# A Trainium2 kernel of two transformer blocks: stage inputs, squares and memory parts placed 64 bytes further in SBUF

## The chip, the cores and the metric

One core of one Trainium2 chip runs the whole program in one launch. The metric is the device time of that core in microseconds (us); lower is better. Before the change it is 3032.66 us, the median of 3 runs (3022.43 to 3038.39).

## The reference, cut to what matters

Everything is float32. The input is x with 256 tokens of 1024 features. A first block runs two layers of (FFN, mixer of four branches, FFN). A second block runs four layers of (mixer, cross-attention over 256 memory tokens, FFN); its mixers are differential attention, HGRN2, a chunked gating unit, and differential attention again. The cost is in products of activations (256 tokens) with weights. The FFN, of which there are eight in all, shows the pattern:

```python
def swiglu(h, w_gu, w_down):
    gate, up = jnp.split(h @ w_gu, 2, axis=-1)
    return (jax.nn.silu(gate) * up) @ w_down
...
        x = x + mem_cross_attention(rmsnorm(x, norm_cross[i]), mem_n, ca_w_q[i], ca_w_kv[i], ca_w_o[i])
        x = x + swiglu(rmsnorm(x, norm_ffn[i]), ffn_w_gu[i], ffn_w_down[i])
```

In each FFN the hidden width is 2816, so the first product has 2 x 2816 output features and the second 2816 input features.

## The kernel before, in words

**Three products for one.** Each float32 operand is cut into a high part, rounded to the type fp32r, and a low part, the rounded remainder. One product of a 128x128 block becomes three matmuls into the same PSUM accumulator, issued by `product` (L432 to L438): low weight or activation part times high (L435), high times low (L436), high times high (L437). Each is one load of a stationary operand (128x128, shown as engine PEld) and one matmul that streams a moving operand of 256 columns (PE). In the profile's names the moving operand stands first and the stationary second: `G<-ah,wl` streams `ah` against loaded `wl`. Projections by `features` (L440) and the FFN's `down` (L569) stream activations against loaded weights; projections by `tokens` (L473) and `tokens_by_input` (L461) stream weights against loaded activations.

**The weights' ring.** The weights come in 460 units of 128x2048 float32 (1 MB) through a ring of five slots. For each unit the SP queue waits until PE has finished the unit five places earlier (`unit_done`, L371) and starts the DMA into `raw` (L372); ACT makes the high part `wh` (L1053) four units ahead of PE; POOL (GpSimd) makes the low part `wl` in place over `raw` (L387); PE waits on `low_ready` and does 48 matmuls for the unit.

**The stages.** Eight FFN stages (`ffn`, L530) have 22 units in the first product, whose moving operands are the stage input parts `ah` and `al`, and 11 units in the second (`down`, L569), whose moving operands are the gated product's parts `gh` and `gl`. Two `mix1` stages, the four mixers and the four cross-attentions use `ah`/`al` for the stage input, `mh`/`ml` for branch outputs or the memory's parts, and `oh`/`ol`, `hoh`/`hol`, `soh`/`sol` for the input of an output projection. At the start of a stage ACT cuts x to `ah` (L1092) and DVE makes `al` (L1688), in four pairs, and PE takes up each pair as it is ready (`features_by_input`, L449). ACT squares x into `full` (L1104) and PE sums those (L514, L517) for the norm, after the second unit of the stage. Evacuations of the first product run on DVE (L1819, L1821, L1824, L1827, L1829) and ACT (L1204).

**Where things lie.** `sb` (L134) hands out byte offsets within each of the 128 partitions, one tensor after the other. All pieces that a matmul or load takes begin at multiples of 512 bytes from the start of their tensor, so that the remainder of a tensor's offset holds for every piece. The program's first free byte is 16481; L141 rounds it up to 16512, which is 129 x 128. With the widths in `sb`'s calls, the offsets of the tensors that matter are:

| tensors | offset before | remainder by 128 | by 256 | offset after | remainder by 128 | by 256 |
|---|---|---|---|---|---|---|
| raw and wl | 16512 | 0 | 128 | 16512 | 0 | 128 |
| wh | 57472 | 0 | 128 | 57472 | 0 | 128 |
| x | 98432 | 0 | 128 | 98432 | 0 | 128 |
| ah | 106624 | 0 | 128 | 106688 | 64 | 192 |
| al | 114816 | 0 | 128 | 114880 | 64 | 192 |
| full | 123008 | 0 | 128 | 123072 | 64 | 192 |
| mh | 131200 | 0 | 128 | 131264 | 64 | 192 |
| ml | 139392 | 0 | 128 | 139456 | 64 | 192 |
| decays (a part of con) | 150912 | 0 | 128 | 150976 | 64 | 192 |
| work: gh, gl, oh, ol and the like | 163648 | 64 | 64 | 163776 | 64 | 192 |
| lh, ll (in work, 32768 further) | 196416 | 64 | 64 | 196544 | 64 | 192 |

The other tensors of `work` (`prob1`, `z`, `cum`, all with remainder 96 by 128) keep their remainder by 128; `ones`, `ident` and the masks go from 0 to 64 with `full`. The last tensor ends at 229312 bytes after the change, under the limit of 229368.

Of the kernel before, what the change touches and what calls it, by code (L numbers as in the profile page):

```python
# [128 lines left out]
def build(nc, w_units, params_d, consts_d, hot_d, rel_d, x_d, mem_d, ws_d, bs_d, out_d,  # L129
          table_d, units=UNITS, stop_after=None):  # L130

    at = [nc.sbuf_base]

    def sb(name, width, dt=F32, offset=None):  # L134

        if offset is None:
            offset = at[0]
            at[0] += (4 * width + 31) // 32 * 32
        return nc.alloc_sbuf_tensor_at(name, [P, width], dt, offset=offset)
# [3 lines left out]
    wl = sb("wl", RING * UW, F32R, offset=at[0] - 4 * RING * UW)  # L143
    wh = sb("wh", RING * UW, F32R)
    x = sb("x", KD * T)
    acts_at = at[0]
    ah = sb("ah", KD * T, F32R)
    al = sb("al", KD * T, F32R)
# [8 lines left out]
    root = sb("root", 4 * T + 8)  # L157
    rr = root[:, 3 * T:4 * T + 2]
    small = sb("small", 136)
    work_at = at[0]  # L160
    WORK = 12288
    work = sb("work", WORK)
# [2603 lines left out]
def program(nc, arrays, **kw):  # L2766
    args = [nc.dram_tensor(k, list(a.shape), F32, kind="ExternalInput").ap() for k, a in arrays.items()]
    args.append(nc.dram_tensor("out", [P, KD * T], F32, kind="ExternalOutput").ap())
    args.append(nc.dram_tensor("tables", [12, P, PERIOD], F32, kind="Internal").ap())
    build(nc, *args, **kw)  # L2770
# [12 lines left out]
```

How the kernel before makes its waits and increments, by code:

```python
        @block.sync  # L356
        def _(sp):
            sp.dma_start(par[:, :], params_d).then_inc(par_in, 16)
            for k in range(KD // 2):
                sp.dma_start(x[:, k * 512:(k + 1) * 512], x_d[:, k * 512:(k + 1) * 512]).then_inc(x_in[k], 16)
            sp.dma_start(raw[:, 0:UW], w_units[0, :, :]).then_inc(raw_landed[0], 16)
            sp.dma_start(onehot[0:NB + 1, :], hot_d).then_inc(tables_in, 16)
            sp.dma_start(rel[0:NB + 1, 0:12], rel_d).then_inc(tables_in, 16)
            for n in range(1, RING):
                sp.dma_start(raw[:, n * UW:(n + 1) * UW], w_units[n, :, :]).then_inc(raw_landed[n], 16)
            sp.dma_start(con[:, :], consts_d).then_inc(consts_in, 16)
            with sp.Fori(1, units // RING) as i:
                for j in range(RING):
                    sp.wait_ge(unit_done, RING * i + (j + 1 - RING))
                    sp.dma_start(raw[:, j * UW:(j + 1) * UW], w_units[i * RING + j, :, :])\
                        .then_inc(raw_landed[j], 16)
            for c2 in range(KD // 2):
                sp.wait_ge(result, c2 + 1)
                sp.dma_start(out_d[:, 512 * c2:512 * (c2 + 1)], full[:, 512 * c2:512 * (c2 + 1)])\
                    .then_inc(stored, 16)
            sp.wait_ge(stored, 16 * (KD // 2))
# [4 lines left out]
            def low(n, j):  # L384
                pool.wait_ge(high_ready, n + 1)
                pool.tensor_tensor(wl[:, j * UW:(j + 1) * UW], raw[:, j * UW:(j + 1) * UW],
```

## Time and profile before

| | us |
|---|---|
| median of 3 runs | 3032.66 |
| lowest and highest run | 3022.43, 3038.39 |
| the profiled execution's own time | 3031.32 |
| its span in the trace | 3029.5 |
| PE busy in it | 2922.5 |
| POOL busy | 2123.0 |
| ACT busy | 1328.3 |
| DVE busy | 1131.8 |

The span is the trace's first to last instruction; 1.8 us of the execution's own time lie outside it. Matmuls overlap their neighbours in the trace: each is shown as lasting some 280 ns while the next begins 110 to 120 ns later, so the pace of PE is read from the starts, not from the durations. The clock column of a window (PEclk) is the share of full TensorE speed that the chip granted, 1.00 for 2.4 GHz and 0.50 for 1.2 GHz.

### The profile page before, as it was taken

What the parts mean: (1) busy time and instruction counts of PE and PEld (TensorE: products, weight loads), DVE (VectorE), ACT (ScalarE), POOL (GpSimd) and SP (SyncE); (2) the same over time, 40 slices, a digit from 0 to 9 for tenths busy, and PEclk for the clock granted to TensorE, in tenths of its full rate; (3) what the DMA queues carried; (4) which work ended last, traced back from release to release, by engine and by line L of the source; (5) the groups of instructions that cost most, each with busy time, mean ns of one, the idle gap of its engine ahead of it and who ended that gap; (6) DMA issues with size and microseconds to landing.
All of it is one profiled execution on the core that took longest, in us unless ns stands there. A gap on an engine that the chain in (4) does not pass through costs nothing.

```text
span 3029.5 us, 56111 instructions
## 1 busy us (share of the span) xinstructions
PE 2922.5 (96%) x24276; PEld 2866.2 (95%) x24276; DVE 1131.8 (37%) x1810; ACT 1328.3 (44%) x1473; POOL 2123.0 (70%) x464
## 2 busy tenths in 40 slices
PE   7999999999999999999999999999998999999998
PEld 7999889999998899999999998999998999999998
DVE  2326544223165343245242226343134431353421
ACT  4344534343345344355443475443354433454432
POOL 5887558778866477866678682668876488756685
PEclk9999989999999899999999999999999999999999
DMA  6554335555544254544345541445553355434453
GB/s 224 190 194 160 140 125 177 185 181 181 192 163 147 105 194 169 195 167 154 140 167 182 181 169 66 144 153 181 181 195 140 126 184 192 170 143 147 158 186 116
DMA packets 73441, 496.89 MB, mean 164 GB/s; under 512 B 8027, under 2 KB 12763, under 8 KB 14084
## 3 DMA queue, kind: packets, MB, share of 16 engines
q1 hardware_dynamic: 67768, 485.88, 45.0%
q10 hardware_dynamic: 5452, 7.62, 1.0%
q8 instruction: 192, 3.15, 0.4%
q14 instruction: 29, 0.24, 0.0%
HBM read 490.05 MB, written 3.41 MB: 163 GB/s over the span
## 4 chain that ended last, share of the span: by engine, by line
PE 85%; DVE 6%; DMA 3%; issue 3%; ACT 2%; POOL 2%; SPq 0%; DVEq 0%; POOLq 0%; ACTq 0%
PE G L435 21%; PE G L436 21%; PE G L437 21%; PE S L437 5%; PE S L435 5%; PE S L436 5%; DMA raw<-w_units 3%; DVE al L1688 3%; POOL wl L387 2%; PE G L634 1%; PE S L983 1%; ACT wh L1053 1%; PE S L514 1%; PE S L517 0%; PE S L782 0%
## 5 line engine op out<-in xcount | busy, mean ns | idle before, releaser
L387 POOL TENSOR_TENSOR wl<-raw,wh 128x2048 fp32r<-128x2048 f32 x460 | 2122.8, 4624 | 877.2 <-ACT wh L1053 862.3
L1053 ACT ACTIVATE wh<-raw 128x2048 fp32r<-128x2048 f32 x456 | 871.6, 1913 | 1096.8 <-DMA raw<-w_units 1096.5
L435 PE MATMUL G<-ah,wl 128*128 128x256 f32 x4304 | 1235.7, 287 | 44.2 <-DVE al L1688 36.0
L436 PE MATMUL G<-al,wh 128*128 128x256 f32 x4304 | 1228.0, 285 | 0.0
L437 PE MATMUL G<-ah,wh 128*128 128x256 f32 x4304 | 1227.4, 285 | 0.0
L435 PEld LDWEIGHTS G<-ah,wl 128*128 128x128 f32 x4304 | 836.0, 194 | 57.2 <-DVE al L1688 28.7
L436 PEld LDWEIGHTS G<-al,wh 128*128 128x128 f32 x4304 | 836.3, 194 | 0.1
L437 PEld LDWEIGHTS G<-ah,wh 128*128 128x128 f32 x4304 | 836.0, 194 | 0.0
L435 PE MATMUL S<-gh,wl 128*128 128x256 f32 x1408 | 388.9, 276 | 0.0
L436 PE MATMUL S<-gl,wh 128*128 128x256 f32 x1408 | 388.9, 276 | 0.0
L437 PE MATMUL S<-gh,wh 128*128 128x256 f32 x1408 | 388.8, 276 | 0.0
L435 PEld LDWEIGHTS S<-gh,wl 128*128 128x128 f32 x1408 | 264.4, 188 | 0.0
L436 PEld LDWEIGHTS S<-gl,wh 128*128 128x128 f32 x1408 | 264.4, 188 | 0.0
L437 PEld LDWEIGHTS S<-gh,wh 128*128 128x128 f32 x1408 | 264.3, 188 | 0.0
L1821 DVE TENSOR_TENSOR G<-G,root 128x512 f32<-128x512 f32 x88 | 61.4, 698 | 369.8 <-PE G L437 369.8
L1850 DVE SCALAR_TENSOR_TENSOR x<-S,x 128x512 f32<-128x512 f32 x32 | 21.9, 685 | 408.8 <-PE S L437 408.8
L1688 DVE SCALAR_TENSOR_TENSOR al<-x,par,ah 128x256 fp32r<-128x256 f32 x144 | 168.3, 1213 | 15.5 <-ACT ah L1092 15.4
L1092 ACT ACTIVATE ah<-x,par 128x256 fp32r<-128x256 f32 x144 | 64.5, 500 | 175.9 <-DVE x L1768 140.9
L1819 DVE TENSOR_TENSOR G<-G,root 128x512 f32<-128x512 f32 x88 | 61.4, 698 | 190.4 <-PE G L437 190.1
L435 PE MATMUL G<-mh,wl 128*128 128x256 f32 x384 | 110.0, 286 | 3.2 <-ACT kc L1171 1.7
L435 PE MATMUL G<-wh,al 128*128 128x256 f32 x384 | 109.2, 284 | 4.0 <-DVE ll L2453 2.2
L436 PE MATMUL G<-wl,ah 128*128 128x256 f32 x384 | 108.7, 283 | 0.0
(357 smaller groups left out, 3873.1 us busy)
## 6 DMA issues: line engine op xcount, KB each, us to landing
raw<-w_units SPq DMA_DIRECT2D x460, 1024.0 KB, 4.8
bias<-tables ACTq DMA_DIRECT2D x24, 128.0 KB, 4.4
tables<-trow ACTq DMA_DIRECT2D x1, 1536.0 KB
con<-consts SPq DMA_DIRECT2D x1, 1056.0 KB, 18.2
x<-x_in SPq DMA_DIRECT2D x4, 256.0 KB, 5.2
memx<-mem_in ACTq DMA_DIRECT2D x1, 1024.0 KB, 4.8
out<-full SPq DMA_DIRECT2D x4, 256.0 KB, 2.5
tables<-trow ACTq DMA_DIRECT2D x1, 768.0 KB
```

The source lines that it names most:

```text
L387: pool.tensor_tensor(wl[:, j * UW:(j + 1) * UW], raw[:, j * UW:(j + 1) * UW], wh[:, j * UW:(j + 1) * UW].bitcast(F32), ALU.subtract)\
L435: pe.matmul(out, sl, vh, start=start and k == 0, stop=False, **kw)
L436: pe.matmul(out, sh, vl, start=False, stop=False, **kw)
L437: ins = pe.matmul(out, sh, vh, start=False, stop=stop and k == len(parts) - 1, **kw)
L514: pe.matmul(out[:, 0:T], ones[:, 0:P], full[:, k * T:(k + 1) * T], start=k == 0, stop=k == 1)
L634: ins = pe.matmul(out, v_of(kc), pt[:, kc * 512 + n * P:kc * 512 + (n + 1) * P], start=kc == 0, stop=kc == nk // P - 1)
L983: ins = pe.matmul(out[:, h * T:(h + 1) * T], qf[:, f * T + g * P:f * T + (g + 1) * P], kc[:, f * T:(f + 1) * T], start=dc == 0, stop=dc == 1)
L1053: act.activation(wh[:, j * UW:(j + 1) * UW], raw[:, j * UW:(j + 1) * UW], ACT.Copy)\
L1092: ins = act.activation(ah[:, q * T:(q + 1) * T], x[:, q * T:(q + 1) * T], ACT.Copy, scale=pcol(gain, q))
L1688: ins = dve.scalar_tensor_tensor(al[:, q * T:(q + 1) * T], x[:, q * T:(q + 1) * T], pcol(gain, q), ah[:, q * T:(q + 1) * T].bitcast(F32), ...
L1819: dve.tensor_tensor(pairs(gate), pairs(gate), along, ALU.mult).then_inc(scaled, 1)
L1821: dve.tensor_tensor(pairs(value), pairs(value), along, ALU.mult).then_inc(up_scaled, 1)
```

## The change

Two lines are added to the layout. The first moves everything from `ah` on by 64 bytes; the second sets the start of `work` to the next offset that leaves 64 by 128, which was its remainder already. No instruction, wait, transfer or size is different; only the addresses are.

```diff
     wl = sb("wl", RING * UW, F32R, offset=at[0] - 4 * RING * UW)
     wh = sb("wh", RING * UW, F32R)
     x = sb("x", KD * T)
+    at[0] += 64
     acts_at = at[0]
     ah = sb("ah", KD * T, F32R)
     al = sb("al", KD * T, F32R)
...
     small = sb("small", 136)
+    at[0] = (at[0] + 63) // 128 * 128 + 64
     work_at = at[0]
```

## Rows read from the trace of the kernel before

**Rows 1.** The page: busy us, share of the span and instructions by engine.
```profile
PE 2922.5 (96%) x24276; PEld 2866.2 (95%) x24276; DVE 1131.8 (37%) x1810; ACT 1328.3 (44%) x1473; POOL 2123.0 (70%) x464
```

**Rows 2.** What PE waited for, over the whole span; us, times, longest.
```profile
PE G L435 <- DVE al L1688: 37.8, 23, 3.4
...
PE G L634 <- DVE pt L1917: 8.7, 4, 3.6
...
PE G L435 <- POOL wl L387: 3.5, 4, 2.0
```

**Rows 3.** PE's instruction groups, shapes apart: busy us, mean ns, idle before.
```profile
L437 PE MATMUL G<-ah,wh 128*128 128x256 f32 x4304 | 1227.4, 285 | 0.0
...
L437 PE MATMUL S<-gh,wh 128*128 128x256 f32 x1408 | 388.8, 276 | 0.0
...
L437 PE MATMUL G<-wh,ah 128*128 128x256 f32 x384 | 108.7, 283 | 0.0
...
L437 PE MATMUL G<-mh,wh 128*128 128x256 f32 x384 | 108.6, 283 | 0.0
...
L437 PE MATMUL G<-oh,wh 128*128 128x256 f32 x384 | 106.7, 278 | 0.0
...
L437 PE MATMUL G<-wh,mh 128*128 128x256 f32 x256 | 72.5, 283 | 0.0
...
L437 PE MATMUL S<-mh,wh 128*128 128x256 f32 x128 | 36.2, 283 | 0.0
```

**Rows 4.** Tile view of ah, gh and oh, one stretch each: count, first and last start.
```profile
L435 PE MATMUL G<-ah,wl x279: 283/283/284, 679.7 to 779.8; 128*128 128x256 f32 x140
...
L435 PE MATMUL S<-gh,wl x119: 275/276/277, 159.8 to 199.9; 128*128 128x256 f32 x119
...
L435 PE MATMUL G<-oh,wl x54: 276/276/277, 1499.8 to 1517.8; 128*128 128x256 f32 x54
```

**Rows 5.** Windows of these stretches: PE busy, then PEclk, DMA share, GB/s.
```profile
680.00:780.00 100.00, 100.00 (x836) 100.00 (x835) 30.59 (x44) 37.30 (x27) 85.33 (x19) 1.00 0.51 182
160.00:200.00 40.00, 40.00 (x356) 40.00 (x355) 0.00 (x0) 15.23 (x8) 33.24 (x8) 1.00 0.53 186
...
1412.00:1432.00 20.00, 20.00 (x172) 20.00 (x172) 7.45 (x8) 8.15 (x9) 11.51 (x4) 1.00 0.56 206
```

**Rows 6.** The tile view of ah where weights stream (1796 to 1812 us).
```profile
L436 PE MATMUL G<-wl,ah x45: 283/283/284, 1795.9 to 1811.7; 128*128 128x256 f32 x45
```

**Rows 7.** Timeline of PE, the first matmuls with decays: start us, us.
```profile
1816.27 0.28 PE L875 MATMUL S<-decays,lh 128*128 128x256 f32 x1
...
1817.97 0.28 PE L876 MATMUL S<-decays,ll 128*128 128x256 f32 x1
```

**Rows 8.** The tile view of oh in the first differential attention (1412 to 1432 us).
```profile
L435 PE MATMUL G<-oh,wl x57: 280/281/282, 1412.1 to 1431.8; 128*128 128x256 f32 x57
```

**Rows 9.** Timeline of PE at an FFN's start at the lower clock: start us, us.
```profile
1718.10 0.41 PE L436 MATMUL G<-al,wh 128*128 128x256 f32 x1
...
1720.66 0.41 PE L436 MATMUL G<-al,wh 128*128 128x256 f32 x1
```

**Rows 10.** The cores view: span in us and mean granted clock.
```profile
core 0: 3029.5 us, clock 0.985
```

**Rows 11.** Windows of the first FFN and the third.
```profile
40.00:110.00 70.00, 66.25 (x544) 65.30 (x544) 20.41 (x31) 23.88 (x18) 46.50 (x11) 1.00 0.68 199
640.00:835.00 195.00, 193.44 (x1641) 193.16 (x1640) 53.10 (x75) 78.94 (x62) 156.37 (x34) 1.00 0.52 184
```

**Rows 12.** The tile view of raw, 700 to 780 us: the supply of weights.
```profile
L387 POOL TENSOR_TENSOR wl<-raw,wh x15: 4614/4621/4634, 696.2 to 775.5; 128x2048 fp32r<-128x2048 f32 x15
...
DMA to landing us min/median/max: 4.7/4.8/7.0
```

**Rows 13.** The tile views of soh and mh: ns min/median/max of their making.
```profile
L1642 DVE TENSOR_TENSOR sol<-full,soh x4: 678/678/4512, 2275.4 to 2281.1; 128x512 fp32r<-128x512 f32 x4
...
L2011 DVE TENSOR_TENSOR ml<-full,mh x4: 691/693/1099, 370.2 to 1056.0; 128x512 fp32r<-128x512 f32 x4
```

## The prediction

> **What bounds the kernel now.** I read the page's busy times first: PE is busy for 2922.5 of 3029.5 us, POOL for 2123.0, ACT and DVE for less than half [rows 1]. The view of waits says how little PE stands still: its largest item is 37.8 us in 23 waits for DVE's `al` at the starts of stages, the others are a few us each [rows 2]. So PE is the bound nearly everywhere, and the question is at what pace it works while it never waits. The durations of the groups hint at an answer: matmuls that stream `ah` or `mh` against weights last 283 to 285 ns, those that stream `gh` 276, those that stream `oh` 278 [rows 3]. As durations overlap, I take the pace from first and last starts. From 679.7 to 779.8 us there are 279 matmuls of L435 on `ah`, each followed by two more of its product: 100.1 us / 278 / 3 = 120.0 ns per matmul. For `gh` it is 40.1 / 118 / 3 = 113.3 ns, for `oh` after 1500 us 18.0 / 53 / 3 = 113.2 ns [rows 4]. PE is busy without a break in the stretches of `ah` and `gh` and the granted clock is 1.00 in both (2.4 GHz), so neither a wait nor the clock makes the difference [rows 5].
>
> What differs is the remainder of the two SBUF operands by 128 bytes. `ah` and the weights both leave 0, `gh` and `oh` leave 64 against the weights' 0. Two more pairs help to tell whether the moving operand alone decides. Where weights stream against a loaded `ah`, again 0 with 0, the pace is 15.8 / 44 / 3 = 119.7 ns [rows 6]. Where `decays` (0) streams against a loaded `lh` or `ll` (64), 16 matmuls start within 1.70 us, 1.70 / 15 = 113.3 ns [rows 7]. It is the pair that counts: equal remainders cost 6.7 ns a matmul, different ones do not, whichever side has the 64. One stretch does not fit: the output projection of the first differential attention also streams `oh`, and runs at 19.7 / 56 / 3 = 117.3 ns [rows 8] at a granted clock of 1.00 [rows 5].
>
> **The change, part by part.** It removes no instruction and adds none. The first line gives `ah`, `al`, `full`, `mh`, `ml` the remainder 64; the second keeps `gh`, `oh` and the rest of the working area at 64. So the pairs of 0 with 0 become 64 with 0.
>
> Their number: per form (4304 + 384 + 384 + 256 + 128) products with `ah` or `mh` on either side = 5456, times three matmuls = 16368 [rows 3]. Not all run at 120 ns. After the wait at a stage's start the clock falls to its lower level, and the matmuls then start 2.56 / 12 = 213 ns apart [rows 9]. The mean clock of 0.985 [rows 10] leaves 0.015 x 2 x 3029.5 = 91 us at the lower level; if all of that were such matmuls it would be some 430. I leave 400 out, as part of it is other work. The gross gain is 15970 x (120.0 - 113.3) = 107 us. In an FFN that is 22 x 48 x 6.7 ns = 7.1 us of some 190 [rows 11].
>
> What of it is lost:
> - *Starts of stages.* There PE takes the pairs of `ah`/`al` as DVE gives them, 23 waits [rows 2]. What PE saves in the first unit, 48 x 6.7 = 0.32 us, partly becomes waiting. Between 0 and 23 x 0.32 = 7.4 us; I take 4, since the first wait is often the long one and the rest of the unit runs free.
> - *Cover inside the mixers.* Units of weights cover the work of DVE and ACT on attention and decays, and PE already waits at the end of some, 4 times for `pt` [rows 2]. With the smaller items of that view I count some 30 such waits. Each loses at most one unit's 0.32 us, 0 to 9.6 in all; I take 3, because most waits last well under 1 us and several follow fp32 matmuls that keep their pace.
> - *The first FFN.* There weights arrive late: PE is busy for 66.25 us of 70 [rows 11]. Units that PE leaves earlier ask for weights earlier, so something between nothing and the whole 7.1 us is lost; I take 3.
> - *Supply elsewhere.* A unit now takes 48 x 120 = 5.76 us of PE and would take 5.44. POOL needs 4.62 per unit and a transfer lands after 4.8 [rows 12]; `down` works at 5.44 per unit already, at 186 GB/s and without a wait [rows 5]. I take 0; if the cover failed, PE would wait for `wl` as in the first FFN (3.5 us in 4 waits [rows 2]).
> - *Pairs that become equal.* `decays` goes to 64 and meets `lh` and `ll` at 64: 128 matmuls x 6.7 = 0.9 us, a loss. `ones` and `full` move together and stay equal; the transposes stream or load fp32, where I see no such pace in the trace and take 0.
> - *DVE and ACT on the moved tiles.* The subtraction that makes `sol` from tiles of different remainder takes 678 ns, that of `ml` from equal ones 693 [rows 13]. So both signs are possible, 15 ns an instruction. Only the first two `al` of a stage lie on the path: under 1 us in all, taken as 0.
>
> The sum: 107 - 4 - 3 - 3 - 1 = 96 us. The profiled execution took 3031.3 us, which gives 2935; its time is 1.4 us under the median shown, so I say **2936**.
>
> A rule speaks against all this. The Trainium skill, in SBUF — State Buffer, section "SBUF: two separate sides", says that TensorE, ScalarE and VectorE's own port pair never wait on anyone, and it names no effect of addresses on the two reads of TensorE. By that rule the change gives 0 and the time stays 3033; the two paces in this trace do not agree with it. A second page, TensorE: Matmul & The Clock Gate, section "Back-to-back issue gap", gives 262 cycles at full clock for 256 columns, an estimate of 109.2 ns; by that the gross gain could be 172 us, but no long stretch here goes under 113.
>
> **The rivals.**
> *Part of PE's time falls into the pace of 117.3 ns* that `oh` shows although its remainders differ [rows 8]. Against it: the eight `down` phases and the other output projections hold 113. If all the moved pairs ran so, the gain would be 15970 x 2.7 = 43 us less 8 of losses, 2998; if half did, 2967.
> *No change.* The pace may hang on something else that separates the tiles, such as how far apart or how high they lie. Then the time stays at 3033. For it: `gh`, `oh`, `lh` all lie in the upper working area. Against it: `decays`, 0 by 128, lies just above `ml` and is fast only because its partner is elsewhere; the rule of the skill would end here too.
> *Slower: the remainder that counts is that by 256.* The weights leave 128, `gh` leaves 64 now and 192 after. If the fast pairs are those where the streamed operand is 64 below the weights, and 64 above is as slow as equal, then `ah` gains nothing and the products with `gh` and the `oh` family fall back: (1408 + 384 + 64 + 64) x 3 = 5760 matmuls x 6.7 = 39 us, a time of 3071. It decides if a streamed operand 64 above its partner is slow. `decays` is 64 above `lh` by 256 and ran at 113.3 [rows 7], but those are only 16 matmuls.
>
> **How the numbers follow.** The main case, the pace of 113 nearly everywhere, gets 0.82; the pace of 117 for much of the work 0.10; no change 0.05; slower 0.03. About 0.5% (15 us) is what a measurement of this kernel can tell from no change. The first two cases are faster by more than that: 0.92. The range: without any loss the profiled 3031.3 - 107 = 2924, and runs of one kernel lie up to 10 us under their median, so 2915; upward the upper bounds of the losses (7.4 + 9.6 + 7.1 + 1 = 25) give 2950, and the case of half the work at 117 gives 2967, so I close at 2976. Left out are full 117, no change and slower, about 0.15.
>
> **What would show it.** In the profile after, the tile view of `ah` in a window of an FFN should give 113.3 ns per matmul and durations of 276; tokens' matmuls the same; `gh` and `oh` as before, `decays` with `lh` 120. An FFN should last 7 us less, PE's busy time fall to about 2820, its waits grow by 5 to 20 us, and POOL's busy time stay at 2123. `ah` at 120 would refute the reading of remainders, `gh` at 120 would show the rule by 256, and a large wait for POOL or DMA would show supply as the next bound.

## The result: 1.6% faster, half of what was forecast

The changed kernel takes 2982.36 us (median of 4 runs, 2981.16 to 2983.62) against 3031.06 us for the kernel before: the ratio is 0.9837, with a 95% interval of 0.9818 to 0.9856. The forecast was 2936 us with a range of 2915 to 2976, so the direction was right and the size, 49 us instead of 95, was not.

The page of the changed kernel (line numbers are two higher than before) shows busy times and the largest groups of PE, then DVE's group for `al`:

```profile
PE 2895.0 (97%) x24276; PEld 2840.8 (95%) x24276; DVE 1105.2 (37%) x1810; ACT 1328.5 (45%) x1473; POOL 2125.6 (71%) x464
...
L439 PE MATMUL G<-ah,wh 128*128 128x256 f32 x4304 | 1207.1, 280 | 0.0
...
L439 PE MATMUL S<-gh,wh 128*128 128x256 f32 x1408 | 393.0, 279 | 0.0
...
L1690 DVE SCALAR_TENSOR_TENSOR al<-x,par,ah 128x256 fp32r<-128x256 f32 x144 | 139.3, 1012 | 12.9 <-ACT ah L1094 12.7
```

Against [rows 1] PE is busy for 27.5 us less, while the matmuls of the group that streams `ah` last 280 ns instead of the 285 of [rows 3], and those of `gh` 279 instead of 276. The paces stand in the tile views, here of `ah` from 700 to 780 us and from 219 to 228 us, of `ah` where weights stream (from 1752 us), and of `gh` from 160 to 200 us:

```profile
L437 PE MATMUL G<-ah,wl x228: 280/280/280, 699.7 to 779.9; 128*128 128x256 f32 x114
...
L437 PE MATMUL G<-ah,wl x28: 276/276/276, 218.7 to 227.9; 128*128 128x256 f32 x28
...
L438 PE MATMUL G<-wl,ah x54: 276/276/276, 1751.8 to 1769.9; 128*128 128x256 f32 x54
...
L437 PE MATMUL S<-gh,wl x114: 279/279/279, 159.8 to 199.7; 128*128 128x256 f32 x114
```

In the long stretches the matmuls on `ah` now start every 80.2 / 227 / 3 = 117.8 ns. Some short stretches, the second row shows one, go at 9.2 / 27 / 3 = 113.6 ns; they hold 850 of the 12912 matmuls that stream `ah`. Streamed weights against a loaded `ah` go at 18.1 / 53 / 3 = 113.8 ns here; and `gh`, which was at 113.3 ns [rows 4], goes at 39.9 / 113 / 3 = 117.7 ns. The granted clock is full in both long stretches, as the windows show:

```profile
700.00:780.00 80.00, 80.00 (x682) 80.00 (x681) 24.90 (x36) 31.13 (x22) 67.10 (x15) 1.00 0.51 185
160.00:200.00 40.00, 40.00 (x342) 40.00 (x341) 0.00 (x0) 13.98 (x8) 32.86 (x8) 1.00 0.52 184
```

The third difference stands in PE's waits. Where 37.8 us in 23 waits went to `al` before [rows 2], the changed kernel has:

```profile
PE G L437 <- DVE al L1690: 12.5, 17, 1.3
...
PE G L636 <- DVE pt L1919: 8.9, 4, 3.8
...
PE G L437 <- POOL wl L389: 6.2, 5, 2.7
```

**The ledger.** I took the distance between the starts of every pair of consecutive matmuls in the two traces. Of the 16368 matmuls on moved tiles some 16000 run without a wait and at full clock; their mean fell from 119.93 to 117.20 ns, a gain of 16000 x 2.73 = 44 us. The 5720 others of the `gh` and `oh` family rose from 113.7 to 117.8 ns, a loss of 23 us. The waits for `al` fell by 25 us. The distances on moved tiles that show the lower clock in whole or in part (131 to 230 ns) fell from 311 to 238; at some 95 ns more than a matmul at full clock that is 7 us. Together 53 us, and the spans differ by 49.7: the waits for POOL grew by 2.7 us [rows 2], and the rest is spread over small items. So only 44 - 23 = 21 us of the gain come from the pace of the matmuls, which is what the change aimed at; 32 us come from the starts of stages.

### The profile page after: what moved, and what is told of

Same layout as the page of the kernel before. It is cut to its first block, busy times and chain, and to the rows that moved or that the text cites. A ratio compares the mean times of both kernels' runs of the same rounds, so it can differ in the third digit from the quotient of the medians.

```text
span 2979.8 us, 56111 instructions
## 1 busy us (share of the span) xinstructions
PE 2895.0 (97%) x24276; PEld 2840.8 (95%) x24276; DVE 1105.2 (37%) x1810; ACT 1328.5 (45%) x1473; POOL 2125.6 (71%) x464
## 4 chain that ended last, share of the span: by engine, by line
PE 85%; DVE 5%; issue 3%; DMA 3%; ACT 2%; POOL 2%; SPq 0%; POOLq 0%; DVEq 0%; ACTq 0%
PE G L437 21%; PE G L439 21%; PE G L438 21%; PE S L437 5%; PE S L439 5%; PE S L438 5%; DMA raw<-w_units 3%; DVE al L1690 2%; POOL wl L389 2%; PE G L636 1%; PE S L985 1%; ACT wh L1055 1%; PE S L516 1%; PE S L519 0%; PE S L784 0%
## 5 line engine op out<-in xcount | busy, mean ns | idle before, releaser
L437 PE MATMUL G<-ah,wl 128*128 128x256 f32 x4304 | 1217.8, 283 | 22.4 <-DVE al L1690 11.3
L438 PE MATMUL G<-al,wh 128*128 128x256 f32 x4304 | 1207.7, 281 | 0.0
L439 PE MATMUL G<-ah,wh 128*128 128x256 f32 x4304 | 1207.1, 280 | 0.0
L437 PEld LDWEIGHTS G<-ah,wl 128*128 128x128 f32 x4304 | 815.8, 190 | 34.5 <-issue 24.4
L439 PEld LDWEIGHTS G<-ah,wh 128*128 128x128 f32 x4304 | 816.1, 190 | 0.0
L438 PEld LDWEIGHTS G<-al,wh 128*128 128x128 f32 x4304 | 813.9, 189 | 0.1
L1690 DVE SCALAR_TENSOR_TENSOR al<-x,par,ah 128x256 fp32r<-128x256 f32 x144 | 139.3, 1012 | 12.9 <-ACT ah L1094 12.7
L437 PE MATMUL G<-oh,wl 128*128 128x256 f32 x384 | 107.8, 281 | 0.0
```

The source lines that it names most:

```text
L437: pe.matmul(out, sl, vh, start=start and k == 0, stop=False, **kw)
L438: pe.matmul(out, sh, vl, start=False, stop=False, **kw)
L439: ins = pe.matmul(out, sh, vh, start=False, stop=stop and k == len(parts) - 1, **kw)
L1690: ins = dve.scalar_tensor_tensor(al[:, q * T:(q + 1) * T], x[:, q * T:(q + 1) * T], pcol(gain, q), ah[:, q * T:(q + 1) * T].bitcast(F32), ...
```

## The experiments

Addresses or small matters of order differ in these kernels, and one (g_entry_mm) has a few matmuls more. The time of each is given with its ratio to the kernel before, run beside it. The expectations name their theories by letters and say what each holds. Distances of tiles are given here by 256 bytes, from the weights, which are never moved: "64 above" for 64 more than the weights, "64 below" for 64 less. In the kernel before `ah` is level with the weights and `gh` 64 below; in the changed kernel both are 64 above. The second line of the change, which keeps 64 by 128, moved `gh` by 128 bytes to the other side.

### The working area alone

```diff
     small = sb("small", 136)
+    at[0] += 128
     work_at = at[0]
```

> Only the working area moves, by 128 bytes: ah leaves 128 by 256 like the weights, gh and oh leave 192. Theory A (side): ah at 120, gh and oh at 117.8, 26 us more than the kernel before, about 3057. Theory B (entry): gh enters from the pace of 120 as before and takes 113.3, about 3031.

Measured: 3023.12 us, ratio 0.9958 (0.9934 to 0.9982), beside 3035.64 for the kernel before. The tile view of `gh` from 160 to 200 us and PE's wait for `al`:

```profile
L436 PE MATMUL S<-gh,wl x114: 280/280/280, 159.8 to 199.7; 128*128 128x256 f32 x114
```

```profile
PE G L436 <- DVE al L1689: 12.9, 17, 1.5
```

As theory A says, `gh` is at 39.9 / 113 / 3 = 117.7 ns, in all eight FFNs, although it is entered from the pace of 120 as before. `ah` stays at 120. So the side on which `gh` lies decides its pace, and the remainder by 128 can't be the whole rule. The time was missed by both theories: matmuls that are 24 us slower in sum gave a kernel 12.5 us faster than before. What paid for it is the wait for `al`, 12.9 us where it was 37.8, without a change to `ah`, `al` or x, and fewer matmuls at the lower clock behind these waits.

**Why slower matmuls shorten that wait** can be followed at the stage that starts near 1520 us. First DVE and POOL in the kernel before, as timelines (start us, us); the second row is the last of the four `al` of the first:

```profile
1520.63 7.88 DVE L1688 SCALAR_TENSOR_TENSOR al<-x,par,ah 128x256 fp32r<-128x256 f32 x4
...
1523.74 4.77 DVE L1688 SCALAR_TENSOR_TENSOR al<-x,par,ah 128x256 fp32r<-128x256 f32 x1
```

```profile
1518.11 4.63 POOL L387 TENSOR_TENSOR wl<-raw,wh 128x2048 fp32r<-128x2048 f32 x1 [0.84 <-ACT wh L1053]
1523.54 9.41 POOL L387 TENSOR_TENSOR wl<-raw,wh 128x2048 fp32r<-128x2048 f32 x2 [0.79 <-ACT wh L1053]
```

then the same place with the working area moved:

```profile
1537.29 3.36 DVE L1689 SCALAR_TENSOR_TENSOR al<-x,par,ah 128x256 fp32r<-128x256 f32 x4
...
1540.16 0.48 DVE L1689 SCALAR_TENSOR_TENSOR al<-x,par,ah 128x256 fp32r<-128x256 f32 x1
```

```profile
1534.55 4.62 POOL L388 TENSOR_TENSOR wl<-raw,wh 128x2048 fp32r<-128x2048 f32 x1 [1.02 <-ACT wh L1054]
1540.20 4.95 POOL L388 TENSOR_TENSOR wl<-raw,wh 128x2048 fp32r<-128x2048 f32 x1 [1.02 <-ACT wh L1054]
```

The four `al` of the last two pairs take 7.88 us in the one and 3.36 in the other. In both, the third pair can't go on before POOL's subtraction ends (1522.74 and 1539.17). In the kernel before POOL starts its next one at 1523.54, 0.20 us ahead of the last `al`, which stands still until it ends. With the other pace the output projection's units are 5.65 us apart instead of 5.44, POOL starts at 1540.20, 0.04 us behind the last `al`, and nothing stands still. PE then also doesn't fall to the lower clock there. The Trainium skill (SBUF — State Buffer, "SBUF: two separate sides") describes this lock: a DVE instruction with two SBUF inputs and a GpSimd instruction that reads SBUF exclude each other for their whole length. The trace agrees: an `al` of 0.47 us lasts 4.77 when POOL is first. The kernel before loses this race at six stage starts, each time by 0.18 to 0.20 us; the changed kernel loses it at none, but wins it at ten of them by only 0.02 us, which is luck and no design.

### The race by itself

In the kernel before, with its own addresses, ACT makes the last owed high part behind the squares, so that POOL is released later (cut to its core):

```diff
-                    if owed[0] and owed[0] >= KD // 2 - k:
+                    if owed[0] and owed[0] >= KD // 2 - k and k < KD // 2 - 1:
                         owed[0] -= 1
                         step()
...
+                if owed[0]:
+                    owed[0] -= 1
+                    step()
                 if unit[0] + LEAD < units:
```

> The kernel before with its own addresses; in cut_input ACT makes the weights' high part that is owed behind the last pair only after the squares, some 2.2 us later, so that POOL's subtraction starts behind DVE's last al. Theory D (a race at the start of six stages: POOL starts 0.2 us before DVE's last pair and holds it up for 3.7 us, and PE then does some 17 matmuls at the lower clock): the waits for al fall from 38 us in 23 to about 13 us, each of the six starts gains 3.7 + 1.6 = 5.3 us, 32 us in all, about 3001. Rival E (the changed addresses themselves made DVE or POOL faster there): nothing changes, about 3033.

Measured: 2996.64 us, ratio 0.9887 (0.9861 to 0.9912), 36.7 us less than the kernel before.

```profile
PE G L435 <- DVE al L1691: 17.3, 17, 2.2
```

The paces are those of the kernel before (`ah` 120.0, `gh` 113.4 in every FFN), and the wait is 17.3 us. So the race alone was worth 37 us of the kernel before. That the changed kernel got most of that by being slower elsewhere is what the ledger's 32 us and the experiment before this one say together; no run takes the race out of the changed kernel itself.

### Both sides for both tiles

`root`, `small` and `pick2` are moved ahead of `ah`; their 4800 bytes bring `ah` 64 below the weights without padding, and `gh` stays 64 below.

```diff
     x = sb("x", KD * T)
+    root = sb("root", 4 * T + 8)
+    rr = root[:, 3 * T:4 * T + 2]
+    small = sb("small", 136)
+    pick2 = sb("pick2", 28)
     acts_at = at[0]
```

> root, small and pick2 are moved ahead of ah; no byte is added. ah, mh and full then leave 64 by 256 (they left 128 before, 192 after the change), the weights 128, the working area with gh and oh 64 as before the change. Theory A, the side counts: a streamed operand 64 below its loaded partner by 256 goes at 113.3 ns, one 64 above at 117.8. Then ah, mh, gh and oh run at 113.3, the products that stream weights at 117.8, and the time is about 2905 to 2930 us, the upper end if the long waits for al of the kernel before return. Theory B, only entry counts: with remainders 64 apart on either side both paces hold once taken, most restarts take 117.8, and gh takes over what ah has. Then ah and gh stand mostly at 117.8 and the time is about 2982. Theory C, the forecast's, equal or not by 128: nothing differs from the changed kernel, 2982.

Measured: 3001.0 us, ratio 0.9901 (0.9869 to 0.9933). None of the three theories holds as it stood. `gh` runs at 40.1 / 118 / 3 = 113.3 ns in four FFNs and at 50.2 / 142 / 3 = 117.8 ns in the other four, and always at the pace that `ah` had just before it. Two of its down phases, the first and the second:

```profile
L435 PE MATMUL S<-gh,wl x119: 276/276/276, 169.8 to 209.9; 128*128 128x256 f32 x119
...
L437 PE MATMUL S<-gh,wh x143: 281/281/281, 599.7 to 649.9; 128*128 128x256 f32 x143
```

Side by side with the other three layouts (paces of the long stretch of `ah` after the norm's sums and of `gh`, by FFN; where PE is stopped on the way, as by late weights in the first FFN or by the memory's sums in the fourth, parts of a stretch can have the other pace):

| kernel | ah | gh | pace of ah, FFNs | pace of gh, FFNs |
|---|---|---|---|---|
| before | level | 64 below | 120.0 in 8 | 113.4 in 8 |
| working area alone | level | 64 above | 120.0 in 8 | 117.8 in 8 |
| the change | 64 above | 64 above | 117.8 in 8 | 117.8 in 8 |
| e_plus_minus | 64 above | 64 below | 117.8 in 8 | 113.4 in 4, 117.8 in 4 |
| e_minus_plus | 64 below | 64 above | 113.3 in 1 and part of 2 others, 117.8 in the rest | 117.8 in 8 |
| e_minus_minus | 64 below | 64 below | 113.3 and 117.8 | 113.3 in 4, 117.8 in 4 |

The median of e_minus_minus is worse than the change's although its matmuls are faster (mean 115.6 ns on the moved tiles): with output projections at 113.3 ns its waits for `al` are 48.5 us.

The next kernel, e_plus_minus, has `ah` 64 above and `gh` 64 below; only `root` and `small` are moved ahead, from behind `pick2`:

```diff
+    root = sb("root", 4 * T + 8)
+    rr = root[:, 3 * T:4 * T + 2]
+    small = sb("small", 136)
     acts_at = at[0]
```

> root and small are moved ahead of ah: ah, mh and full leave 192 by 256 as in the changed kernel, the working area with gh and oh stays at 64 as in the kernel before. Theory A (side): ah at 117.8, gh and oh back at 113.3, 5760 matmuls x 4.5 ns = 26 us less than the changed kernel, about 2956. Theory B (entry): gh enters from ah at 117.8 and stays there, about 2982. Theory C: 2982.

Measured: 2999.86 us, ratio 0.9899 (0.986 to 0.9937). Half of the down phases hold 113.4 ns after an `ah` at 117.8, so neither theory is right alone. Both missed the time, which is longer than the change's although `gh` and `oh` are faster in the mean (115.3 ns against 117.8) and the moved tiles no slower: the waits for `al` are back at 36.6 us, and six `al` last 4.8 us again.

The last of the four, e_minus_plus, has `ah` 64 below and `gh` 64 above: the four lines of e_minus_minus, and:

```diff
+    at[0] += 128
     work_at = at[0]
```

> root, small and pick2 ahead of ah and 128 bytes before the working area: ah leaves 64 by 256, gh and oh leave 192. Theory A (side): ah at 113.3; gh is 64 above, so 117.8, unless it can hold the 113.3 that it enters with. 2982 less about 52 us for ah = 2930 with gh at 117.8, 2911 with gh at 113.3. Theory B (entry): about 2982.

Measured: 2972.26 us (2971.54 to 2972.97, 2 runs only), ratio 0.9791 (0.9769 to 0.9813), a little faster than the change (0.9837, 0.9818 to 0.9856) and far from theory A's 2930, since most of `ah` did not take 113.3. In the second FFN of the trace `ah` runs at 113.4 ns (100.0 / 294 / 3), and the `gh` that follows, 64 above, goes at 50.1 / 142 / 3 = 117.6:

```profile
L436 PE MATMUL G<-ah,wl x295: 276/276/276, 484.7 to 584.7; 128*128 128x256 f32 x148
...
L438 PE MATMUL S<-gh,wh x143: 279/279/279, 589.8 to 639.9; 128*128 128x256 f32 x143
```

### The late high part with both tiles 64 below

The four lines of e_minus_minus, and the edit of the race:

```diff
-                    if owed[0] and owed[0] >= KD // 2 - k:
+                    if owed[0] and owed[0] >= KD // 2 - k and k < KD // 2 - 1:
```

> The kernel with ah and gh both 64 below the weights by 256 (e_minus_minus, 3001 us), plus the later high part as in f_late. Theory D: its nine blocked starts lose their 3.7 us waits and most of the half-clock matmuls, 9 x 5.3 = 48 us, about 2953; paces of the matmuls as in e_minus_minus, give or take what chance gives. Rival E: about 3001.

Measured: 2955.55 us (2952.96 to 2956.91), ratio 0.9752 (0.9729 to 0.9776), 2.6 us from what theory D gave. Its waits for `al` are 17.1 us. But only the first two FFNs of this trace are at 113.3 ns, the others at 117.8.

### What decides between 113.3 and 117.8

First the order of the norm's sums, on e_minus_plus:

```diff
-                for k in range(2):
-                    pe.matmul(out[:, 0:T], ones[:, 0:P], full[:, k * T:(k + 1) * T], start=k == 0, stop=k == 1)
                 for tb in range(TB):
                     for k in range(2):
...
+                for k in range(2):
+                    ins = pe.matmul(out[:, 0:T], ones[:, 0:P], full[:, k * T:(k + 1) * T], start=k == 0, stop=k == 1)
```

> e_minus_plus (2972 us) with the two parts of row_sums exchanged: the four matmuls of one column come first, the two of 256 columns last, so that the products after the norm's sums are entered from a full-width matmul. Theory F (with ah 64 below, both paces hold once taken, and the entry decides): most of ah after the sums runs at 113.3 instead of half of it, some 6500 matmuls x 4.5 ns = 29 us, about 2943. Rival G (what runs beside PE decides, not the entry): about half at either pace again, about 2972.

Measured: 2975.71 us (2966.39 to 2985.29), ratio 0.9818 (0.9781 to 0.9854). Inconclusive for the time: more of `ah` is at 113 ns than in e_minus_plus (some 7100 matmuls against 5000), but the runs spread over 19 us, and the choice still falls one way or the other from FFN to FFN: 113.3 after the sums in five FFNs, 117.8 in three.

Then an entry from the pace of 120, on f_late_mm:

```diff
                     else:
+                        if u == 2:
+                            s = (n0 + j) % RING
+                            for _ in range(6):
+                                pe.matmul(G[(g0 + j) % 4][:, 0:T], wcut(wl, s, 0, P), wcut(wh, s, 0, 256),
+                                          start=True, stop=True)
                         ins = features(G[(g0 + j) % 4], (n0 + j) % RING, ah, al)
```

> f_late_mm (ah and gh 64 below the weights by 256, the later high part, 2955.5 us) with six matmuls more ahead of the third unit of each FFN: they stream wh against a loaded wl, both with remainder 0, into the bank that the unit then overwrites, so that the unit is entered from the pace of 120 ns, as gh is in the kernel before. They are no part of the result. Theory F (both paces hold once taken and what runs before decides; from 120 a pair with the streamed side 64 below falls to 113.3, as gh did in eight FFNs of eight before): all eight FFNs run ah after the norm's sums and gh at 113.3; of some 7000 ah and 3200 gh matmuls at 117.8 most become 113.3, about 40 us, less 48 x 0.12 = 6 us for the matmuls added, about 2921. Rival G (entry does not matter, chance or what runs beside PE decides): the same mixture as in f_late_mm, 2955 + 6 = 2961.

Measured: 2938.17 us (2935.34 to 2958.98), ratio 0.9702 (0.9649 to 0.9755), the fastest kernel of this study. Six matmuls that stream weights against weights stand ahead of an FFN's third unit, in a PSUM tile that the unit then overwrites. Here is `ah` in the FFN that starts after 1500 us, first in f_late_mm, then with the entry, and below it the last FFN with the entry:

```profile
L435 PE MATMUL G<-ah,wl x227: 281/281/281, 1519.9 to 1599.7; 128*128 128x256 f32 x114
```

```profile
L435 PE MATMUL G<-ah,wl x236: 276/276/276, 1520.0 to 1599.9; 128*128 128x256 f32 x118
...
L435 PE MATMUL G<-ah,wl x284: 281/281/281, 2749.8 to 2849.8; 128*128 128x256 f32 x142
```

From 79.8 / 226 / 3 = 117.7 ns it went to 79.9 / 235 / 3 = 113.3. Seven of eight entries gave 113.4 ns, where two had done so without it (8838 of the 12912 matmuls that stream `ah` start 111 to 115 ns behind the one before, against 4695); the eighth (last row, 100.0 / 283 / 3 = 117.8) did not. In one FFN the sums for the memory's norm stop the stream at its fourteenth unit, and it goes on at 117.8. The time was 17 us short of the forecast, which had nearly everything at 113.3.

That the pace of 120 at the entry draws `ah` to 113.3 is not shown by this. The traces hold a simpler order that theory F did not look at: the pace that `ah` has just ahead of the sums. Here it is in the second and the fifth FFN of f_late_mm, with `ah` behind the sums of the second between them (behind those of the fifth stands above, 117.7), and then ahead of the sums of the fifth and the last FFN of g_entry_mm:

```profile
L435 PE MATMUL G<-ah,wl x17: 281/281/281, 466.8 to 472.4; 128*128 128x256 f32 x17
...
L435 PE MATMUL G<-ah,wl x30: 276/276/276, 478.0 to 487.8; 128*128 128x256 f32 x30
...
L435 PE MATMUL G<-ah,wl x18: 276/276/276, 1500.0 to 1505.8; 128*128 128x256 f32 x18
```

```profile
L435 PE MATMUL G<-ah,wl x19: 276/276/276, 1496.8 to 1502.9; 128*128 128x256 f32 x19
...
L435 PE MATMUL G<-ah,wl x17: 281/281/281, 2736.0 to 2741.7; 128*128 128x256 f32 x17
```

Without the six matmuls the stream comes out of the sums at the other pace: from 117.8 to 113.3 or from 113.3 to 117.8, in all eight FFNs of each of the four kernels with `ah` 64 below (e_minus_minus, e_minus_plus, f_late_mm, f_swap_mp), 32 of 32. With the six matmuls it comes out at the pace that it went in with, in eight of eight: seven at 113.3, and the last, which went in at 117.8, at 117.8. So in an FFN the pace ahead of the sums, with whether the six matmuls stand behind them, tells the pace that follows in all 40 cases. This is read from the traces; no run changed the pace ahead of the sums by itself, and in the mixers and cross-attentions most sums show the same change, but not all.

### Other distances

Each moves other tiles ahead of `ah`: `root` in e_32, `root` and `small` with 32 bytes more in e_96, `root` and `pick2` in e_160, `pick2` in e_128. The edit of e_96 is:

```diff
+    root = sb("root", 4 * T + 8)
+    rr = root[:, 3 * T:4 * T + 2]
+    small = sb("small", 136)
+    at[0] += 32
     acts_at = at[0]
```

> Only root is moved ahead of ah: ah, mh and full leave 32 by 128 (160 by 256), the weights 0 (128), gh and oh as in the kernel before. Theory H (the pair is slow only where both remainders fall into the same half of 128 bytes): ah runs at 120 as in the kernel before, 3031. Theory J (any difference moves it off 120): paces between 113 and 118, the time 2985 to 3010.

Measured: 3011.75 us, ratio 0.9918 (0.9885 to 0.9952).

> root and small ahead of ah and 32 bytes of padding: ah, mh, full leave 96 by 128 (224 by 256, 96 above the weights), gh and oh 96 by 128 too (96 by 256, 32 below the weights). Theory K (only the distance by 128 counts, with a sign: 32 above gave 116.7, 32 below gave 118.3 in e_32): ah and gh both at 118.3, the weights streamed against ah at 116.7; 16368 x 1.9 = 31 us gained and 5760 x 4.9 = 28 us lost against the kernel before, and without the pace of 113 in the output projections no blocked starts, -32: about 3000. Rival L (the distance by 256 counts): ah, 96 above, at another pace than gh, 32 below.

Measured: 3019.16 us, ratio 0.9943 (0.9921 to 0.9965).

> root and pick2 ahead of ah: ah, mh, full leave 32 by 128 as in e_32, but 32 by 256 where e_32 has 160, that is 96 below the weights instead of 32 above; gh and oh as in the kernel before. Theory K (only the distance by 128 counts): ah at 116.7 and the weights streamed against ah at 118.3, as in e_32, and the time of e_32, 3012 or up to 15 less. Rival L (by 256): ah at another pace.

Measured: 3019.37 us, ratio 0.9942 (0.9919 to 0.9966).

> Only pick2 (128 bytes) is moved ahead of ah: ah, mh and full leave 0 by 128 like the weights, but 0 by 256 where the weights leave 128; gh and oh as in the kernel before. Theory K (the distance by 128 counts, as the forecast said): ah at 120 as in the kernel before, about 3031. Rival L (the distance by 256 counts, as 96 above at 120 and 96 below at 117.3 suggest): ah at a pace clearly off 120 in long stretches.

Measured: 3026.93 us, ratio 0.9966 (0.9947 to 0.9986). The tile view of `ah` from 490 to 590 us, in the second FFN, in these four in this order:

```profile
L435 PE MATMUL G<-ah,wl x287: 277/280/280, 489.8 to 589.9; 128*128 128x256 f32 x144
```

```profile
L436 PE MATMUL G<-ah,wl x278: 278/280/283, 490.0 to 589.8; 128*128 128x256 f32 x139
```

```profile
L435 PE MATMUL G<-ah,wl x285: 277/280/282, 490.0 to 589.9; 128*128 128x256 f32 x143
```

```profile
L435 PE MATMUL G<-ah,wl x282: 279/281/285, 489.9 to 589.9; 128*128 128x256 f32 x141
```

In ns per matmul: 32 above 100.1 / 286 / 3 = 116.7; 96 above 99.8 / 277 / 3 = 120.1; 96 below 99.9 / 284 / 3 = 117.3; 128 away 100.0 / 281 / 3 = 118.6. In e_160 two FFNs hold 120.0, and the `gh` that follows them, 64 below as in the kernel before, does not take 113.4 but 50.1 / 142 / 3 = 117.6 ns. Here are `ah` and `gh` in the fifth FFN of e_160:

```profile
L435 PE MATMUL G<-ah,wl x223: 282/283/283, 1559.8 to 1639.7; 128*128 128x256 f32 x112
```

```profile
L435 PE MATMUL S<-gh,wl x143: 281/281/281, 1669.8 to 1719.9; 128*128 128x256 f32 x143
```

So an entry from 120.0 does not always give a `gh` 64 below the faster pace. `gh` 32 below, in e_96, ran at 118.3 in all FFNs. A distance of 32 above and one of 96 below are the same by 128, and so are level and 128 away; their paces differ (116.7 and 117.3, 120.0 and 118.6). The rule is not one of remainders by 128, and no distance tried gave less than 113.3. Theory J holds for the pace in e_32, and the time is 2 us above its range; theory K falls with e_96, where `ah` was to be at 118.3, and with e_160 and e_128. The small gains of the last three kernels are sums of both effects. In e_128 the mean on the moved tiles is 1.2 ns lower, 19 us on 16000 matmuls, but the waits for `al` are 45.7 us instead of 37.8. In e_96 the matmuls are slower in sum (`gh` and `oh` by 27 us), and the kernel gains through its waits for `al`, 11.8 us where they were 37.8.

## Why the prediction was wrong, point by point

- *What bounds the kernel*: right. PE stayed the bound, at full clock, and its pace in unbroken stretches is what the addresses change. Supply held: the waits for POOL are 6.2 us, and POOL's busy time 2126 us.
- *"Equal remainders cost 6.7 ns a matmul, different ones do not, whichever side has the 64"*: this is the step that failed. The gross term of 107 us came out as 44: the moved pairs went to 117.2 ns in the mean, not 113.3. The prediction had one stretch of 117.3 ns before it [rows 8] and treated it as an exception. The starts of all the 170 matmuls of that stretch give 117.8 ns: it was the second pace that a pair 64 apart can hold, and the changed layout takes it almost everywhere. The row that was to carry the claim for 64 above, 16 matmuls of `decays` [rows 7], lasted 1.8 us, too short a stretch for that. PE's busy time fell to 2895 us and not to about 2820.
- *"The second keeps `gh`, `oh` and the rest of the working area at 64"*, costed at nothing: wrong by 23 us. By 256 it moved them from below to above, and the working area moved by itself shows their fall to 117.8 ns. The slower rival had this mechanism and its price of 39 us; it happened, at 4.1 instead of 6.7 ns a matmul, together with the gain it was meant to exclude (the prediction gave it 0.03).
- *Starts of stages*, a loss of 4 us: wrong in sign. The waits for `al` fell by 25 us and the matmuls at the lower clock by 7. The prediction saw 23 waits and asked what a faster PE would lose there; the long ones among them were made by POOL and DVE, started 0.2 us apart, and hang on the pace of the output projection ahead of them. Without these 32 us the gain would have been some 17 us: that the time came out as low as it did owes more to this luck than to the pace that was forecast.
- *Pairs that become equal*: `decays` with `lh` and `ll`, level in the changed kernel, start 1.78 / 15 = 118.7 ns apart where it was 113.3, near the 120 of the sum. *Cover, first FFN, DVE and ACT*: a few us; nothing in the traces contradicts them, and no run tests them one by one. The rule of the Trainium skill (SBUF — State Buffer, "SBUF: two separate sides") that TensorE never waits on anyone was rightly not used to put the change at nothing: at a granted clock of 1.00 long stretches of `ah` went from 120.0 to 117.8 ns by the addresses alone. The rule itself is about engines that wait for each other, and no run here speaks against that.
- *The rivals*: the first, all moved pairs at 117.3 and 2998 us, had the right pace for them, and a gain of 43 us where 44 were measured. It had no loss on `gh` (23 us) and no gain at the starts (32 us), which in part cancel. It had been given 0.10. The range closed at 2976, 6 us too low.

## What to carry to other kernels

When a layout is changed, look at the distance between the two operands that a matmul stream reads at the same time, not at each address, and look at what every other tile behind the inserted bytes lands on: here the tiles that "kept" their alignment gave back 23 of the 44 us that the moved ones gained. A pace read from one long stretch may be one of two that the same addresses allow, so compare all stretches of a tile before a gain is multiplied by thousands of matmuls. And a wait at a stage's start that is decided by 0.2 us can be worth more than the edit that shifts it: give the instruction that must win a clear lead, as the late high part did for 37 us.

## What the runs showed of the hardware that was not expected

- With the weights and the streamed activations in SBUF at the same width, type and full clock, the pace of fp32r matmuls of 256 columns took values of 113.3, 116.7, 117.3, 117.8, 118.3, 118.6 and 120.0 ns, in kernels in which only addresses differ. It hangs on the pair and not on the streamed operand alone: weights streamed from the same addresses against a loaded `ah` went from 120.0 ns in the mean in the kernel before to 114.2 in the changed kernel, where `ah` lies elsewhere.
- At a distance of 64 the stream has two paces, 113.3 and 117.8 ns. It keeps the one it has for hundreds of matmuls, and with both tiles 64 below also from `ah` to `gh`; a break, or a stream with another distance ahead of it, can change it. Other distances have a second pace too: behind the memory's sums e_32 goes on at 117.8 instead of 116.7, and e_128 at 120.0 instead of 118.6. With `ah` level, only 120.0 was seen.
- With `ah` 64 below, the norm's sums turn one pace into the other in 32 of 32 FFNs, and with six matmuls of weights against weights behind them they leave it as it was in eight of eight. With `gh` 64 below, an entry from 120.0 gave 113.4 in all 16 FFNs of the kernel before and f_late, but 117.8 in the two of e_160.
- Open: what within the reads makes the difference, and why the sums turn the pace. The weights stayed in place in all runs, so that a distance from them and a tile's own remainder by 256 are told apart by nothing longer than the 16 matmuls of `decays`. Whether more than the remainder by 256 matters was not tried by itself. Offsets finer than 32 bytes were not tried either.
